# The hybrid layers' MLP: a shared turn of the last feature tile in the down product, and squares added tile by tile on VectorE

## What is computed

```python
def rmsnorm(x, g):
    y = x * lax.rsqrt(jnp.mean(x * x, axis=-1, keepdims=True) + EPS)
    return y * g

def hybrid_layer(x, ...):
    h = rmsnorm(x, g_mix)
    z = h @ w_in                      # 512 x 1024 @ 1024 x W_IN
    ...                               # attention, retention, gates
    x = x + mixed @ w_out
    h2 = rmsnorm(x, g_mlp)
    x = x + jnp.square(jax.nn.relu(h2 @ w_up)) @ w_down     # 1024 -> 4096 -> 1024
    return x
```

## Time and profile before

| | |
|---|---|
| median of 3 runs | 3530.44 us (3522.07 to 3534.06) |
| the profiled execution | 3525.57 us, span 3523.6 us |
| PE (TensorE matmul) busy | 3413.9 us, 97% of the span |
| PEld (weight load) | 2795.0 us, 79% |
| POOL (GpSimd) | 1777.8 us, 50% |
| DVE (VectorE) | 1578.6 us, 45% |
| ACT (ScalarE) | 1212.5 us, 34% |
| mean granted clock of TensorE | 0.979 |

### The profile page before, as it was taken

The page is one execution under the profiler, slowest core; times in us unless marked ns, Lnnn a source line. Parts: engine busy times, 40 slices in busy tenths (PEclk is TensorE's granted clock), DMA queues, the critical chain, the costliest instruction groups (busy, mean ns, idle before and its releaser), DMA issues.

```text
span 3523.6 us, 49760 instructions
## 1 busy us (share of the span) xinstructions
PE 3413.9 (97%) x17418; PEld 2795.0 (79%) x17418; DVE 1578.6 (45%) x2511; ACT 1212.5 (34%) x1967; POOL 1777.8 (50%) x2019
## 2 busy tenths in 40 slices
PE   8999999999999999999999999999999899999998
PEld 6678887887767887887788878888888787878887
DVE  4533257777544227777845444411212545442212
ACT  4333242223333333323433453312212334543322
POOL 5325567776433556779454213333334354246555
PEclk9999999999999999999899999999999999999999
DMA  4112235443211224444332112112111332132223
GB/s 145 60 43 96 95 131 178 163 165 120 77 61 55 98 99 176 168 172 143 117 106 78 49 43 102 50 64 66 60 62 64 101 104 72 55 114 97 99 96 101
DMA packets 98543, 347.43 MB, mean 99 GB/s; under 512 B 10528, under 2 KB 18976, under 8 KB 96480
## 3 DMA queue, kind: packets, MB, share of 16 engines
q1 hardware_dynamic: 70560, 257.20, 21.7%
q10 hardware_dynamic: 27840, 88.29, 7.3%
HBM read 336.86 MB, written 8.59 MB: 98 GB/s over the span
## 4 chain that ended last, share of the span: by engine, by line
PE 80%; issue 9%; DVE 6%; POOL 2%; ACT 2%; ACTq 1%; DVEq 0%; DMA 0%; POOLq 0%; SPq 0%
PE ps L954 8%; PE ps L953 8%; PE ps L955 8%; PE ps L637 6%; PE ps L638 6%; PE ps L639 6%; PE ps L895 3%; PE ps L896 3%; PE ps L897 3%; POOL w_lo L522 2%; PE ps L661 2%; PE ps L1021 2%; PE ps L1022 2%; PE ps L1023 2%; PE ps L662 2%
## 5 line engine op out<-in xcount | busy, mean ns | idle before, releaser
L522 POOL TENSOR_TENSOR w_lo<-w_raw,w_hi 128x256 fp32r<-128x256 f32 x1904 | 1658.3, 902 | 1694.4 <-ACT w_hi L1355 1680.3
L1355 ACT ACTIVATE w_hi<-w_raw 128x1024 fp32r<-128x1024 f32 x472 | 499.3, 1058 | 846.2 <-PE ps L955 349.2
L637 PE MATMUL ps<-h_hi,w_hi 128*128 128x512 f32 x944 | 377.2, 400 | 0.0
L638 PE MATMUL ps<-h_lo,w_hi 128*128 128x512 f32 x944 | 370.9, 393 | 0.0
L639 PE MATMUL ps<-h_hi,w_lo 128*128 128x512 f32 x944 | 370.4, 392 | 0.0
L1021 PE MATMUL ps<-c_hi,w_hi 128*128 128x512 f32 (+1 forms) x832 | 306.3, 368 | 14.1 <-DVE c_lo L2232 7.0
L2117 DVE SCALAR_TENSOR_TENSOR ada_junk<-ada_w,c_silu 128x1024 f32<-128x1024 f32 x192 | 310.9, 1620 | 3.3
L1022 PE MATMUL ps<-c_lo,w_hi 128*128 128x512 f32 (+1 forms) x832 | 290.7, 349 | 0.0
L1023 PE MATMUL ps<-c_hi,w_lo 128*128 128x512 f32 (+1 forms) x832 | 289.8, 348 | 0.0
L953 PE MATMUL ps<-c_hi,w_hi 128*128 128x512 f32 (+1 forms) x768 | 274.8, 358 | 5.7 <-DVE c_lo L2232 5.7
L954 PE MATMUL ps<-c_lo,w_hi 128*128 128x512 f32 (+1 forms) x768 | 275.3, 358 | 0.0
(11 more groups left out here) (359 smaller groups left out, 6059.4 us busy)
## 6 DMA issues: line engine op xcount, KB each, us to landing
w_raw<-in_w SPq DMA_DIRECT2D x476, 512.0 KB, 3.4
ada_w<-in_ada ACTq DMA_DIRECT2D x96, 512.0 KB, 5.6
m_row<-m_spill ACTq DMA_DIRECT2D x16, 384.0 KB, 5.3
wq_row<-wq_spill ACTq DMA_DIRECT2D x16, 384.0 KB, 5.6
x_spill<-x ACTq DMA_DIRECT2D x2, 2048.0 KB, 7.5
bias<-in_rpb ACTq DMA_DIRECT2D x8, 512.0 KB, 4.4
x<-x_spill ACTq DMA_DIRECT2D x2, 2048.0 KB, 8.3
m_row<-m_spill ACTq DMA_DIRECT2D x16, 256.0 KB, 5.0
```

The lines of the kernel that those rows point to most:

```text
L522: last = nc.gpsimd.tensor_tensor(w_lo[:, j, c], w_raw[:, j % RAW, c], w_hi[:, j, c].bitcast(F), ALU.subtract)
L637: nc.tensor.matmul(bank, w_hi[:, j, w], rhs_hi[:, k, :], start=(k == 0), stop=False)
L638: nc.tensor.matmul(bank, w_hi[:, j, w], rhs_lo[:, k, :], start=False, stop=False)
L1355: nc.scalar.activation(w_hi[:, j, :], w_raw[:, j % RAW, :], ACT.Copy).then_inc(hi_ready, 1)
```

## The change

Two things. In `down`, the first two chunks of a group leave their last hidden tile until both have done tiles 0 to 6; then tile 7 of chunk 0 and of chunk 1 follow, each raising chunk_used. In the norm before the MLP, VectorE adds the squares of tiles 1 to 6 to tile 0's in the loop that adds the mixer's output to x, and TensorE sums two tiles (that sum, and tile 7) instead of five. The norm before the mixer stays as it was; its adds move from `root` to ahead of it.

```diff
+        ADDS = KT - HALF_KT - 1 + KT - 2
...
-            def sums(n):
-                for k in range(HALF_KT + 1):
-                    if k < HALF_KT:
-                        pe.wait_ge(sq_ready, n * KT + (k + 1))
-                    else:
-                        pe.wait_ge(sq_added, (n + 1) * (KT - HALF_KT - 1))
-                    for t in range(TT):
-                        last = nc.tensor.matmul(ps[:, 4, t:t + 1], squares[k][:, t * P:(t + 1) * P], ones[:, 0:1],
...
+            def sum_tile(tile, first, end):
+                for t in range(TT):
+                    last = nc.tensor.matmul(ps[:, 4, t:t + 1], tile[:, t * P:(t + 1) * P], ones[:, 0:1],
...
+            def sums_mlp(l):
+                pe.wait_ge(sq_added, l * ADDS + ADDS)
+                sum_tile(squares[0], True, False)
+                pe.wait_ge(sq_ready, 2 * l * KT + 2 * KT)
+                sum_tile(squares[KT - 1], False, True).then_inc(sq_used, 1)
...
                 first_chunk(g0 + G_MLP, 0, 2 * l + 1)
-                sums(2 * l + 1)
+                sums_mlp(l)
...
                 def down(q):
                     with pe.Fori(0, 2) as i:
-                        for j in range(RING):
-                            arrive(g0 + q * 4 + i + (G_MLP + 2), j)
-                            for k in range(KT):
+                        def blocks(j, tiles):
+                            for k in tiles:
                                 pe.wait_ge(ulo_ready, l * N_MLP + q * KT + (k + 1))
...
-                            last.then_inc(chunk_used, 1)
+                            return last
+                        for j in range(2):
+                            arrive(g0 + q * 4 + i + (G_MLP + 2), j)
+                            blocks(j, range(KT - 1))
+                        for j in range(2):
+                            blocks(j, (KT - 1,)).then_inc(chunk_used, 1)
+                        for j in range(2, RING):
+                            arrive(g0 + q * 4 + i + (G_MLP + 2), j)
+                            blocks(j, range(KT)).then_inc(chunk_used, 1)
...
+            def add_square(a, tiles, ready, added):
+                dve.wait_ge(sq_ready, ready)
+                if a >= 2:
+                    dve.wait_ge(sq_added, added)
+                nc.vector.tensor_tensor(tiles[0], tiles[0], tiles[a], ALU.add).then_inc(sq_added, 1)
...
                     if k:
                         lower(2 * l + 1, k - 1, gain_mlp)
+                    if k >= 2:
+                        add_square(k - 1, squares, (2 * l + 1) * KT + k, l * ADDS + (KT - HALF_KT - 1 + k - 2))
                 lower(2 * l + 1, KT - 1, gain_mlp)
```

More of the change, by code:

```diff
@@ L668, in chunk, with sums_mix @@
                 product(g, j, ps[:, j, :], rhs_hi, rhs_lo).then_inc(chunk_used, 1 + pads)
-            def sums(n):
-                for k in range(HALF_KT + 1):
-                    if k < HALF_KT:
-                        pe.wait_ge(sq_ready, n * KT + (k + 1))
-                    else:
-                        pe.wait_ge(sq_added, (n + 1) * (KT - HALF_KT - 1))
-                    for t in range(TT):
-                        last = nc.tensor.matmul(ps[:, 4, t:t + 1], squares[k][:, t * P:(t + 1) * P], ones[:, 0:1],
-                                                start=(k == 0 and t == 0), stop=(k == HALF_KT), skip_group_check=True)
-                last.then_inc(sq_used, 1)
+            def sum_tile(tile, first, end):
+                for t in range(TT):
+                    last = nc.tensor.matmul(ps[:, 4, t:t + 1], tile[:, t * P:(t + 1) * P], ones[:, 0:1],
+                                            start=(first and t == 0), stop=end, skip_group_check=True)
+                return last
+            def sums_mix(l):
+                for k in range(HALF_KT):
+                    pe.wait_ge(sq_ready, 2 * l * KT + (k + 1))
+                    sum_tile(squares[k], k == 0, False)
+                pe.wait_ge(sq_added, l * ADDS + KT - HALF_KT - 1)
+                sum_tile(squares[HALF_KT], False, True).then_inc(sq_used, 1)
+            def sums_mlp(l):
[3 more added lines that the diff above has]
+                sum_tile(squares[KT - 1], False, True).then_inc(sq_used, 1)
             def spread(n):
@@ L705, in _ @@
                 pe.wait_ge(c0_loaded, 16)
-                sums(2 * l)
+                sums_mix(l)
                 chunk(g0, 1, h_hi, h_lo)
@@ L1867, in spread @@
                         one.rearrange("p (t o) -> p t o", o=1).broadcast_to([P, TT, P]), ALU.mult)
[L1869 to L1875, removed]
+            def add_square(a, tiles, ready, added):
[3 more added lines that the diff above has]
+                nc.vector.tensor_tensor(tiles[0], tiles[0], tiles[a], ALU.add).then_inc(sq_added, 1)
             def root(n):
-                add_squares(n, squares[HALF_KT:])
                 dve.wait_ge(std_ready, n + 1)
@@ L1915, in _ @@
                 dve.wait_ge(layer_vec, l * 4 + 4)
+                for a in range(1, KT - HALF_KT):
+                    add_square(a, squares[HALF_KT:], 2 * l * KT + (HALF_KT + a + 1), l * ADDS + (a - 1))
                 root(2 * l)
```

## The result

The kernel became **slower**: 3560.7 us median of 4 runs (3558.15 to 3562.11) against 3528.74 (3522.07 to 3534.06) of the kernel before on the same chip, a ratio of 1.0092 with a 95% interval of 1.0076 to 1.0108. The forecast was 3529.3 us, with a range of 3518 to 3540. The profiled executions stand 36.5 us apart: span 3560.1 us against 3523.6, mean granted clock 0.972 against 0.979.

The account below looks back on a forecast made before the run. TensorE, busy 97% of the span, was taken as the bound, with VectorE on the path at layer ends. Terms -5.3 - 2.7 + 5.1 + 1.7 = -1.2 us gave 3529.3 us, range 3518 to 3540.

Parts of the forecast that it names:

- Sums: Norm before the MLP: 16 sum records instead of 40, 2.63 us less in each layer, -5.3 us.
- Squares on VectorE: Norm before the MLP: six adds a layer in place of three, covered by VectorE's waits, cost 0.
- Tile 7: Down products: the wait before tile 7 gets covered; the first three of each layer give -2.7 us.
- Layer ends: Last down group of each layer: chunk 0 released 4.76 us later costs +5.1 us in layer 0, +1.7 in layer 1.
- Chunk 0's late release in quarters 0 to 2: Down groups there: release 4.76 us later is caught up, cost 0; bounds 0 and 6 x 2 us.
- C: Rival: late mod copy ending each layer's first three down products delays the up phase; about 3541 us, chance 0.08.
- B: Rival: TensorE decides throughout, so sums, tile 7 and perhaps slow stretches gain fully; -17, 3513 us, chance 0.13.
- D: Rival: in the down product tile 6 keeps the large wait and nothing is hidden; 3535 us, chance 0.05.

Follow-up runs that it names:

- late split: Kernel before, with only ScalarE's split into chunk 0's buffer waiting until chunk 1 of a down group is done: 3545.85 us, 1.0052.
- shared turn in the first group only: Changed kernel, with tile 7 put off for chunks 0 and 1 only in the first group of each down product: 3552.41 us, 1.0063.
- short products: VectorE's adaLN products over 128 of 1024 columns: changed kernel 3488.83 us, 0.9891; kernel with only the new sums 3489.17 us, 0.9898.
- small loads and the sums only: Changed kernel with the old down order, adaLN loads bringing 64 of 1024 columns (all but the first three of each layer): 3521.55 us, 0.9978.
- late release without the new order: Kernel before, matmuls in their old order, with chunk 0 of a down group released together with chunk 1: 3568.56 us, 1.0114.
- late add: Kernel before, with only VectorE's add of chunk 0 waiting until chunk 1 of a down group is done: 3565.13 us, 1.0100.
- late add with the loads behind: VectorE's add of chunk 0 waits for chunk 1, in the kernel before with adaLN loads issued behind the fourth chunk's work: 3537.73 us, 1.0034.

## Why the prediction was wrong, point by point

*Sums: right.* 16 records from 488.45 to 490.16 are 1.71 us (forecast 1.75). Timeline of TensorE, changed kernel, and the window from 489.20 to 492.60 (busy of PE, PEld, DVE, ACT, POOL; granted clock, DMA share, GB/s):

```profile
488.45 0.95 PE L675 MATMUL ps<-c,stage 128*128 128x1 f32 x8
489.26 1.03 PE L675 MATMUL ps<-c,squares 128*128 128x1 f32 x8
490.16 0.49 PE L639 MATMUL ps<-h_hi,w_hi 128*128 128x512 f32 x1
```

```profile
489.20:492.60 3.40, 3.40 (x21) 2.95 (x22) 1.03 (x3) 2.24 (x3) 0.00 (x0) 1.00 1.02 412
```

No slow stretch follows, where the clock stood at 0.51 behind 4.38 us of such matmuls. The rule of the Trainium skill that the prediction weighed (TensorE: Matmul & The Clock Gate, Part 1), that activity releases the throttle, agrees with this place. The gain behind it was waited away as forecast, since VectorE sets the first down product: its tile 6 starts at 538.06 instead of 540.65, 2.6 us earlier.

*Squares on VectorE: right*, no wait of TensorE in the norm before the MLP, and the kernel with only the sums gained.

*Tile 7: right as to the wait.* No down product waits before it. That its 2.7 us are gained isn't measured by itself.

*Layer ends: the stall is right in layer 0.* The stall forecast at "about 6 us" before tile 6 of layer 1's first chunk:

```profile
874.92 0.80 PE L654 MATMUL ps<-h_hi,w_hi 128*128 128x512 f32 x1 [6.00 <-DVE h_lo L1906]
```

1.77 us stood there before. With +5.1 there and -2.6 of the sums the stretch from tile 6 to tile 6 was to grow by 2.5 us and grew by 1.5. The price isn't pinned down better than that: the same stretch took 573.28 us with the new down product alone, 1.7 more than before, and 564.57 with the sums only, 8.5 less than in the changed kernel. In layer 1 TensorE now waits 1.95 us for the last square; the +1.7 us forecast there can't be checked inside the scatter of what follows.

*Chunk 0's late release in quarters 0 to 2: wrong, and this is the step that failed.* The prediction put it so: "I estimate its read of the next up chunk as 1 us late, since it had some 2 us to spare there; but the next tile of VectorE had waited 2.34 us for ScalarE, so that is caught up. I take 0; the bounds are 0 and 6 x 2 us." Measured: 5.1 us a passage on average, 30.4 in all. The step failed in three places.

1. *The size.* "Some 3.2" us of lateness at the copy of mod were 4.3 (from 0.2 us ahead of the down product's end to 4.1 behind).
2. *Slack counted for one reader only, and one group only.* VectorE's holes were real and did take up VectorE's share: before the first tile of quarter 1's up product it idled 4.53 us before and 1.96 in the changed kernel, before the second 2.34 and 1.12. But the weights have no such hole. The split feeds GpSimd, GpSimd frees the raw buffer, and that frees SyncE's next load. The prediction named ScalarE's read of the up chunk and left out the weights behind it; of GpSimd it looked only at its distance of 11.6 us from TensorE in the release group. The late split alone, with VectorE on time, lost 20 us. The copy of mod holds the split up as well, since that stands behind the loads in ScalarE's list: 586.69 us where it stood at 584.30, and against the down product's end 4.3 us later. Nor is it enough to look at the second group's copy, as the prediction did: with the shared turn in the first group only, that copy was in time and the passages lost as much.
3. *GpSimd's price by its mean.* 4 x 0.90 us a chunk was taken. In this stretch, beside VectorE's products, 16 pieces took 19.41 us, 4.85 us a chunk. So the stream of weights had little room to come back: TensorE's chunk takes 5.44 us. VectorE is slowed too: over three quarters of layer 0 its product went from 1599 to 1670 ns a piece and w_lo from 1122 to 1191 (first GpSimd before, then changed):

```profile
L522 POOL TENSOR_TENSOR w_lo<-w_raw,w_hi 128x256 fp32r<-128x256 f32 x193 | 210.6, 1122 | 60.5 <-ACT w_hi L1355 60.0
```

```profile
L524 POOL TENSOR_TENSOR w_lo<-w_raw,w_hi 128x256 fp32r<-128x256 f32 x193 | 223.5, 1191 | 62.7 <-ACT w_hi L1376 62.5
```

The Trainium skill (SBUF — State Buffer, Who interferes with whom) says that a VectorE operation with two inputs in SBUF and a GpSimd operation that reads it exclude one another on a shared pair of ports. Both rows getting longer together agrees with that, and so do the 806 ns of w_lo beside short products; no run here isolates it. Longer rows alone are not the loss: in the kernel with small loads and the sums only they are 1179 ns (w_lo, 537.5 to 806.3 us) and 1669 (product), and its passages take 0.8 us more than before.

*The rivals.* C (VectorE's lateness goes round the quarters) had the right sign and witness, "tile-6 waits longer by 2 us in quarters 1 to 3", and a chance of 0.08. Its price, 2 us six times, was 5.1. Its place, the copy of mod at the end of the down product, is one way and not the only one: it too stopped at ScalarE's read of the up chunk. B and D fell: no wait stands before tile 7, and TensorE doesn't decide.

*What is shown and what isn't.* Shown: the late release alone causes the loss (late release without the new order). Both its readers carry it, each by itself (late split, late add). The late release of the first group is enough for the passages' loss, with the copy at the end of the down product in time (shared turn in the first group only, one profile). Without VectorE's long products there is no loss, and with small adaLN loads it is smaller by a third to somewhat over half. Read from one passage's timeline, and only argued as the general path: copy, split, w_lo, raw load behind adaLN loads, split, relu, u_lo. Open: how the loss divides between VectorE's own list, GpSimd slowed beside it, and transfers that queue behind each other. The late add with the loads behind was meant to separate the first from the others and left a wait on the copy in ScalarE's list. Not tried: a split and a relu that wait for no adaLN load at all, with loads issued from another queue.

## What to carry to other kernels

Before a release is moved later, list every engine that waits on it, and follow each one's list to the end of the cycle: slack found at one reader says nothing of another that stands behind an in-order list or a load. Slack also has to be measured in the stretch where the work meets other work, since a mean over the kernel (0.90 us for a w_lo piece) hides the 1.2 us that it costs where VectorE is busy beside it. And an issue that waits for something unimportant must not stand ahead of something that matters: moving the adaLN loads behind one split and one relu gave 0.6%, more than either half of the change aimed at.

## What the runs showed of the hardware

*Identical code, different time.* Behind the last down product the two kernels run the same instructions. From 1694.00 us before, and from 1721.00 us in the changed kernel, the windows show the same 10199 matmul records (columns as above):

```profile
1694.00:3523.60 1829.60, 1758.93 (x10199) 1479.59 (x10197) 665.29 (x1136) 635.70 (x1071) 764.96 (x935) 0.97 0.25 80
```

```profile
1721.00:3560.00 1839.00, 1770.43 (x10199) 1491.40 (x10197) 671.20 (x1141) 637.94 (x1074) 769.06 (x939) 0.96 0.24 80
```

TensorE is busy 11.5 us longer on as many records, at a granted clock lower by about 0.01. From the last matmul of the last down product to the end, where all kernels of this document have the same code, the 17 profiled executions took between 1829.8 and 1842.3 us, at mean granted clocks of 0.972 to 0.964. From tile 6 of that product on, the kernel before and the one with the sums only run the same matmuls and took 1873.8 and 1884.6 us; the changed kernel and the one with the down product only took 1881.0 and 1873.9. The 7.2 us that the changed kernel lost there lie within this and are put down to no part of the change; they fit the 12 us by which runs of the kernel before differ.

*A transfer's time depends on what was issued just ahead of it.* The same 512 KB of weights landed 4.5 us after its issue when issued just ahead of three adaLN loads of 512 KB, and 6.8 us after it when just behind them. The median of all such loads is 3.5 us.

*The clock.* Behind the waits of 3.70 and 4.53 us before tile 6 (631.77, 538.06) the granted clock was 0.50, the 1.2 GHz level, from 632.60 to 635.50 and from 538.06 to 543.00; the 1.7 us of thin matmuls in the sums did not bring that. The length of a wait alone doesn't tell: in the kernel before, 1.21 us before tile 6 at 720.31 was followed by 1.00, and 1.32 us at 809.43 by 0.50 from 811.40 to 814.70.
